# Cross attention of a decoder step: prompt tiles and sample batches in one alternating order, memory keys turned in the projection ahead

## The chip, the cores and the metric

One core of one Trainium2 chip runs the whole program. The metric is device microseconds (us) of that core; lower is better. TensorE (PE, with its weight loads PEld), VectorE (DVE), ScalarE (ACT), GpSimd (POOL) and SyncE (SP, which only issues DMAs here) each run their own instruction list in order and meet at semaphores.

## The reference, cut to what matters

The kernel computes one layer of a decoder for a prompt (512 tokens, 1024 wide) and for 8 sample batches of 8 tokens each. The change lies in its second part, the cross attention into 256 memory tokens with 4 heads of 256:

```python
def memory_attend(h, mk, mv, w_mq, g_q_mem, w_mo):
    q = rmsnorm((h @ w_mq).reshape(B, L, 4, 256), g_q_mem)
    s = jnp.einsum('blhd,bmhd->bhlm', q, mk).astype(F32) * (256 ** -0.5)
    p = jax.nn.softmax(s, axis=-1)
    o = jnp.einsum('bhlm,bmhd->blhd', p, mv.astype(F32)).reshape(B, L, D_MODEL)
    return o.astype(h.dtype) @ w_mo
```

The prompt attends to keys and values projected in this step from `mem_prompt` (they are outputs too); each sample batch attends to keys and values of its own, read from a cache in HBM (256 x 1024 floats each, 1 MB of keys and 1 MB of values a batch, 16 MB in all).

## The kernel before, in words

The program is a row of stages, each a block that all engines enter and leave together: input projection, mixing (retention and windowed attention), output projection, memory projection, `project_cross` (queries), `cross_attend`, `project_back` (the product with `w_mo`), routing, experts. All numbers are float32. Where accuracy allows the fast matrix path, a float32 matrix is split into a high and a low part of type fp32r and three products are summed; the sample batches' own products and all turns (transposes on PE) are plain float32.

`project_cross` (L1300) calls the helper `dense` (L156), which runs the products k = 0 to 9: two blocks of 512 weight columns, each over five row tiles (four of 128 prompt tokens, one of 64 sample tokens). It uses PSUM banks 0 to 3 for products and 4, 5 for turning the inputs, and calls hooks of ACT, DVE and PE after each product. `wide_norm` (L1252) hangs the per-head norm of the queries there: ACT squares (L1266), DVE reduces (L1274), POOL makes the factor (L1293, L1295), DVE scales (L1285, L1286).

`cross_attend` (L1310) then has two halves, one after the other.

The prompt half: fourteen turn groups of four 128 x 128 turns each (`turns`, L1342, issued at L1376): eight of the prompt's queries, four of the memory keys, two of the samples' queries. They go through four PSUM banks; ACT writes the high part (L1490 is the line of its copy helper, so all its copies have it), DVE the low part (L1557) or a plain copy (L1554). ACT and DVE also split the memory values (L1497, L1569). Then for each tile of 128 queries, with the names that are used below:
- S(t): 24 matmuls of scores into banks 2 and 3 (L1388)
- M(t): DVE takes the maxima (L1563, L1565); E(t): ACT makes the exponentials and their sums (L1504); N(t): DVE normalizes (L1573, L1574)
- TP(t): PE turns the probabilities, 8 turns into banks 4 and 5 (L1402), ACT and DVE split them (L1490, L1579)
- O: after every second tile, 48 matmuls with the values (L1415) into banks 6, 7, 0, 1, evicted by ACT in four parts

S(t+1) is issued ahead of TP(t). S has to wait until E of the tile before has read the banks.

The cache half runs the 8 sample batches in loops. For each batch n:
- K(n): 16 turns of the batch's keys in four groups (L1431) into banks 0 and 1, evicted by DVE (L1591) and ACT into one buffer `skt`
- CS(n): scores, small matmuls of 32 columns of queries (L1441); CM(n): maximum on DVE (L1595, L1597); CE(n): exponential on ACT (L1536); CT(n): turn of the probabilities (L1449); CP(n): their eviction on DVE (L1602)
- CV(n): product with the values (L1456); CN(n): normalization on DVE (L1604, L1607); CO(n): turn of the output (L1464); CW(n): its eviction on DVE (L1610)

The order on PE is K(n+1), CT(n), CV(n), CS(n+1), CO(n). SP first stores the two memory outputs, then loads two batches of keys and values; each later load waits until the batch two before has been read (L1361, L1363). The last thing in SP's list is the first 2 MB of `w_mo` (L152, called at L1366); it waits for the O products (L1365), because it overwrites the turned probabilities.

Of the kernel before, what the change touches and what calls it, by code (L numbers as in the profile page):

```python
# [41 lines left out]
P = 128  # L42
# [1257 lines left out]
def project_cross(nc, m, a):  # L1300

    qm = m.at("cross_q", m.Z, [NT, D])
    m.cross_q = qm
    store = lambda act, bank, b, t: act.activation(qm[:rows(t), t, 512 * b:512 * b + 512], bank[:rows(t), :], ACT.Copy)
    widths = [rows(t) for t in range(NT)]
    hooks = wide_norm(nc, m, "cross", None, qm, m.g_q_mem, NT, widths)
    dense(nc, m, "cross", m.x, m.w_mq, range(NT), store, hooks, m.g_cross, widths, m.Z + 10240)


def cross_attend(nc, m, a):  # L1310

    qm, mk, mv = m.cross_q, m.mem_k, m.mem_v
    qt = m.at("cross_q_t", m.Z + 9216, [C8, T])
    sk = [m.at(f"cache_k{i}", m.W + 2048 * i, [2, D]) for i in range(2)]
# [3 lines left out]


    qt_hi, qt_lo = m.at("cross_q_hi", m.HTH, [C8, SEQ], F32R), m.at("cross_q_lo", m.Z + 9216, [C8, T], F32R)  # L1320
    kt_hi, kt_lo = m.at("mem_k_hi", m.Z + 15872, [C8, MEM], F32R), m.at("mem_k_lo", m.Z + 9216 + C8 * T, [C8, MEM], F32R)
    mv_hi, mv_lo = m.at("mem_v_hi", m.Z + 5120, [2, D], F32R), m.at("mem_v_lo", m.Z + 7168, [2, D], F32R)
    pt_hi, pt_lo = (m.at(f"cross_probs_t_{n}", m.Z + 2048 * i, [2 * MH, 2 * P], F32R) for i, n in enumerate(("hi", "lo")))
    spb = [m.at(f"cache_probs{i}", m.WH + 5120 + 256 * i, [MEM]) for i in range(2)]
    S = m.sem
    tr_done, tr_hi, tev = S("cr_turned"), S("cr_turned_hi"), S("cr_turns_out")
    mv_split, pt_h = S("mem_v_split"), S("cr_p_hi")
    sc_done, mx_done, ex_done, pn_done = S("cr_scored"), S("cr_max"), S("cr_exped"), S("cr_normed")
    pt_done, pt_ev, o_done, o_ev = S("cr_p_turned"), S("cr_p_stored"), S("cr_out"), S("cr_out_stored")
    kin, vin = [S("cache_k0_in"), S("cache_k1_in")], [S("cache_v0_in"), S("cache_v1_in")]  # L1330
    qs = m.at("cache_q", m.WH + 5888, [C8, 32])
    ps = m.at("cache_probs_turned", m.WH + 6144, [2, P])
    so = m.at("cache_out", m.WH + 6400, [MD])
    so_done, st_done = m.sem("cs_out_normed"), m.sem("cs_out_turned")
    cq_done = S("cache_q_done")
    ch, stores = S("cr_chain"), S("cr_stores")
    kt_done, kt_ev = S("ck_turned"), [S("ck_stored_even"), S("ck_stored_odd")]
    s_sc, s_mx, s_ex, s_rl = S("cs_scored"), S("cs_max"), S("cs_exped"), S("cs_recip")
    s_pt, s_pev, s_o, s_oev = S("cs_p_turned"), S("cs_p_stored"), S("cs_out"), S("cs_out_stored")
    ckv = [a[n].rearrange("a b (t p) h d -> p (a b) t (h d)", p=P) for n in ("cache_mem_k", "cache_mem_v")]  # L1340

    turns = [(qm, qt_hi, qt_lo, t, j) for t in range(NT - 1) for j in range(2)] + \  # L1342
        [(mk, kt_hi, kt_lo, t, j) for t in range(2) for j in range(2)] + [(qm, None, qt, NT - 1, j) for j in range(2)]
    TURN_BANKS = (0, 1, 6, 7)
    OUT_BANKS = (6, 7, 0, 1)
    four = lambda ap: ap.rearrange("p (c n) -> p c n", c=4)
    NQ = NT - 1
    SC = MD ** -0.5

    with nc.Block() as block:  # L1350
        @block.sync
        def _(sp):
            for src, dst in ((mk, "o_mk"), (mv, "o_mv")):
                sp.dma_start(a[dst].rearrange("a b (t p) h d -> p (a b t) (h d)", p=P), src[:]).then_inc(stores, 16)
            for b in range(2):
                sp.dma_start(sk[b][:], ckv[0][:, b]).then_inc(kin[b], 16)
                sp.dma_start(sv[b][:], ckv[1][:, b]).then_inc(vin[b], 16)
            with sp.Fori(0, NB // 2 - 1) as i:
                for b in range(2):
                    nxt = bass.ds(i * 2 + 2 + b, 1)  # L1360
                    sp.wait_ge(kt_done, i * 8 + 4 * b + 4)  # L1361
                    sp.dma_start(sk[b][:], ckv[0][:, nxt].rearrange("p a t n -> p (a t) n")).then_inc(kin[b], 16)
                    sp.wait_ge(s_o, i * 2 + b + 2)  # L1363
                    sp.dma_start(sv[b][:], ckv[1][:, nxt].rearrange("p a t n -> p (a t) n")).then_inc(vin[b], 16)
            sp.wait_ge(o_done, 4 * (NQ // 2))  # L1365
            m.w_mo.load(sp)  # L1366
            sp.wait_ge(stores, 32)

        @block.tensor
        def _(pe):  # L1370
            for k, (src, _, _, t, j) in enumerate(turns):
                r = rows(t) if src is qm else P
                if k >= 4:
                    pe.wait_ge(tev, k - 3)
                for c in range(4):
                    last = pe.transpose(m.bank[TURN_BANKS[k % 4]][:, c * P:c * P + r],  # L1376
                                        src[:r, t, (4 * j + c) * P:(4 * j + c + 1) * P], m.ident[:r, :r])
                last.then_inc(tr_done, 1)
            pe.wait_ge(tev, len(turns))

            def scores(t):
                if t:
                    pe.wait_ge(ex_done, 4 * t)
                for h in range(MH):
                    o = m.bank[2 + h // 2][:, (h % 2) * MEM:(h % 2 + 1) * MEM]
# [6 lines left out]
            scores(0)  # L1392
            for t in range(NQ):
                if t + 1 < NQ:
                    scores(t + 1)
                pe.wait_ge(pn_done, t + 1)
                if t:
                    pe.wait_ge(pt_ev, 2 * t)
# [5 lines left out]
                if t % 2 == 0:  # L1404
                    continue
# [3 lines left out]
                if t > 1:  # L1409
                    pe.wait_ge(o_ev, 4 * (t // 2))  # L1410
# [959 lines left out]
```

## Time and profile before

| | us |
|---|---|
| median of three runs (lowest to highest) | 1192.34 (1188.83 to 1197.03) |
| the profiled execution's own time | 1192.52 |
| its span, first to last instruction | 1190.7 |
| mean granted TensorE clock, share of full | 0.886 |
| TensorE busy in the span | 931.5 (78%) |
| VectorE, ScalarE busy | 530.2 (45%), 358.0 (30%) |

The span leaves out 1.8 us around the program. The granted clock is the share of 2.4 GHz that TensorE was given; it takes the levels 0.5 (1.2 GHz) and 1.0, and a number between is a mean over time. The rows further down are of three kinds: stretches of the span with each engine's busy time, groups or single instructions in order of their start, and the times that a DMA took from issue to landing. "x8" means eight instructions merged into a row; what stands in brackets is how long the engine had been idle and what ended it.

### The profile page before, as it was taken

To read this page: it belongs to the slowest core of one execution; us is meant where nothing else is said; L and a number is where in the kernel's file an instruction comes from. 1 tells how busy PE (TensorE), PEld (TensorE's weight loads), DVE (VectorE), ACT (ScalarE), POOL (GpSimd) and SP (SyncE) were. 2 spreads that over 40 slices of the span, in tenths; PEclk is the share of its full clock that TensorE was granted. 3 is DMA by queue.
4 is the path that set the end of the run, shared out by engine and by line. 5 is a ranking of instruction groups with operands and counts; after the bars stand their busy time and mean duration, and the time that the engine had idled before them with its cause. 6 is when DMAs were issued, how large, how long until landed. Compare 5 with 4: busy or idle time off the path is not lost. (4 is left out here: it accounts for less than half of the span.)

```text
span 1190.7 us, 14646 instructions
## 1 busy us (share of the span) xinstructions
PE 931.5 (78%) x5762; PEld 653.6 (55%) x5762; DVE 530.2 (45%) x876; ACT 358.0 (30%) x638; POOL 114.7 (10%) x138
## 2 busy tenths in 40 slices
PE   3989999987777777796969777659762999877881
PEld 2877888864554454685758666438652443322330
DVE  3366467335455444335545553454145334223324
ACT  4532234123444444425355243233130011000010
POOL 1000015421000000000212300000010111111000
PEclk9999999967999888797979978999955899888996
DMA  7111217074777665522440050676085699999967
GB/s 247 37 41 65 72 71 167 32 263 124 221 223 220 202 196 160 187 71 71 142 141 1 6 207 1 247 278 252 7 316 229 241 419 420 420 419 422 420 276 254
DMA packets 80132, 231.83 MB, mean 195 GB/s; under 512 B 23104, under 2 KB 23744, under 8 KB 65600
## 3 DMA queue, kind: packets, MB, share of 16 engines
q1 hardware_dynamic: 73008, 220.66, 51.7%
q0 software_dynamic: 4608, 9.45, 2.1%
q10 hardware_dynamic: 2448, 0.80, 0.3%
q8 instruction: 46, 0.75, 0.3%
q14 instruction: 22, 0.18, 0.0%
HBM read 219.46 MB, written 18.74 MB: 200 GB/s over the span
## 5 line engine op out<-in xcount | busy, mean ns | idle before, releaser
L1952 PE MATMUL bank<-gate_up,slot_rows_t 128*64 128x512 f32 x512 | 126.2, 649 | 27.2 <-DMA gate_up<-w_exp_up 25.3
L1952 PEld LDWEIGHTS bank<-gate_up,slot_rows_t 128*64 128x64 f32 x512 | 41.8, 150 | 109.4 <-issue 76.2
L358 PE MATMUL bank<-in_wh,in_hth 128*128 128x512 f32 x224 | 90.7, 405 | 3.1 <-DVE in_wl L302 3.1
L359 PE MATMUL bank<-in_wl,in_hth 128*128 128x512 f32 x224 | 88.9, 397 | 0.0
L360 PE MATMUL bank<-in_wh,in_htl 128*128 128x512 f32 x224 | 88.7, 396 | 0.0
L2159 DVE TENSOR_TENSOR slot_rows_t<-bank,g_moe 128x512 f32<-128x512 f32 x32 | 20.7, 686 | 148.7 <-PE bank L1946 148.7
L862 PE MATMUL bank<-ident,k_half 128*128 128x128 f32 x320 | 53.1, 309 | 26.0 <-ACT window_k_t L992 17.0
L1966 PE MATMUL bank<-down,hidden_t 128*64 128x512 f32 x256 | 58.5, 597 | 8.4 <-issue 7.3
L862 PEld LDWEIGHTS bank<-ident,k_half 128*128 128x128 f32 x320 | 38.7, 154 | 42.5 <-ACT window_k_t L992 22.4
L2112 ACT ACTIVATE swish<-bank 128x256 f32<-128x256 f32 x16 | 6.2, 385 | 177.8 <-PE bank L1952 177.8
L358 PEld LDWEIGHTS bank<-in_wh,in_hth 128*128 128x128 f32 x224 | 43.2, 193 | 12.8 <-issue 3.5
L360 PEld LDWEIGHTS bank<-in_wh,in_htl 128*128 128x128 f32 x224 | 43.0, 192 | 9.4
L359 PEld LDWEIGHTS bank<-in_wl,in_hth 128*128 128x128 f32 x224 | 43.1, 192 | 8.6
L302 DVE TENSOR_TENSOR in_wl<-in_w,in_wh 128x1024 fp32r<-128x1024 f32 x28 | 32.4, 1219 | 21.1 <-ACT in_wh L235 21.1
L435 ACT ACTIVATE z<-bank 128x512 f32<-128x512 f32 (+1 forms) x35 | 20.5, 589 | 69.3 <-PE bank L360 58.0
L1123 DVE COPY window_k_t<-bank 128x512 f32<-128x512 f32 x40 | 27.5, 688 | 29.3 <-PE bank L862 29.3
L970 ACT ACTIVATE probs<-scored,att_max 128x128 f32<-128x128 f32 (+3 forms) x32 | 17.7, 554 | 74.4 <-DVE att_max L1108 74.4
L1966 PEld LDWEIGHTS bank<-down,hidden_t 128*64 128x64 f32 x256 | 20.2, 136 | 35.6 <-issue 35.6
L208 POOL TENSOR_SCALAR stat<-stat 128x1 f32<-128x1 f32 (+1 forms) x12 | 3.0, 248 | 332.3 <-ACT mem_normed L224 263.1
L235 ACT ACTIVATE in_wh<-in_w 128x1024 fp32r<-128x1024 f32 x28 | 27.3, 1045 | 21.2 <-DMA in_w<-w_in 21.2
L1936 POOL DMA_INDIRECT slot_rows<-moe_rows_dram,slot_token x16 | 16.5, 1029 | 160.6 <-PE bank L1946 104.4
L358 PE MATMUL bank<-wo_wh,wo_hth 128*128 128x512 f32 x64 | 26.2, 410 | 5.9 <-DVE wo_wl L302 5.9
(386 smaller groups left out, 2048.9 us busy)
## 6 DMA issues: line engine op xcount, KB each, us to landing
gate_up<-w_exp_gate SPq DMA_DIRECT2D x32, 1024.0 KB, 21.2
gate_up<-w_exp_up SPq DMA_DIRECT2D x32, 1024.0 KB, 24.9
down<-w_exp_down SPq DMA_DIRECT2D x32, 1024.0 KB, 23.1
in_w<-w_in SPq DMA_DIRECT2D x7, 2048.0 KB, 8.3
k_half<-cache_win_k SPq DMA_DIRECT2D x48, 256.0 KB, 6.2
v_half<-cache_win_v SPq DMA_DIRECT2D x48, 256.0 KB, 4.9
k_half<-cache_win_k SPq DMA_DIRECT2D x8, 1024.0 KB, 6.0
v_half<-cache_win_v SPq DMA_DIRECT2D x8, 1024.0 KB, 8.4
```

Of the source, the lines that this page charges most:

```text
L235: act.activation(wh[b % 2][:, part(i)], w[b % 2][:, part(i)], ACT.Copy).then_inc(wh_done, 1)
L302: dve.tensor_tensor(wl[b % 2][:, part(i)], w[b % 2][:, part(i)], wh[b % 2][:, part(i)].bitcast(F32), ALU.subtract).then_inc(wl_done, 1)
L358: pe.matmul(o, hi, wh[b % 2][:, c, :], start=(c == 0), stop=False)
L359: pe.matmul(o, hi, wl[b % 2][:, c, :], start=False, stop=False)
L360: last = pe.matmul(o, lo, wh[b % 2][:, c, :], start=False, stop=(c == C8 - 1))
L435: return act.activation(z[ZB[b]][:rows(t), t, :], bank[:rows(t), :], ACT.Copy)
L862: last = pe.transpose(m.bank[KBANK[c % 2]][:, q * P:(q + 1) * P], win.k[part][:, c % HC, q * P:(q + 1) * P], m.ident[:, :])
L970: act.activation(pb[:, e, :n], sb[:, e, :n], ACT.Exp, bias=m.amx[:, c], accum_out=m.asum[:, c]).then_inc(ex_done, 1)
L1123: dve.tensor_copy(kt[:, :, c * P:(c + 1) * P], m.bank[KBANK[0]][:].rearrange("p (q n) -> p q n", q=NP)).then_inc(kt_ev[0], 1)
L1952: last = pe.matmul(bank[64 * h:64 * h + 64, :], B.xt[k % 2][:, c, 64 * h:64 * h + 64], B.gu[k % 3][h][:, :, c, :], start=(c == 0), stop=(c ...
L1966: last = pe.matmul(m.bank[4 + j][64 * h:64 * h + 64, :], B.hidt[n % 2][:, k, 64 * h:64 * h + 64], B.dn[n % 3][h][:, k, 512 * j:512 * j + 5 ...
L2159: dve.tensor_tensor(B.xt[k % 2][:, 4 * j:4 * j + 4, :], four(m.bank[j][:]), over(m.g_moe[:, 4 * j:4 * j + 4], P), ALU.mult).then_inc(xt_ev, 1)
```

## The change

In `project_cross`, the four turn groups of the memory keys, their split and the split of the memory values are hung into the hooks: a turn group behind each of the products k = 4 to 7 (PE, into banks 6 and 7, free there; ACT and DVE each one part of the split), half of the values' split behind k = 7 and k = 8. SP's list of this stage gets the stores of the two memory outputs and, once five products are done, the loads of the keys of batches 0 and 1.

In `cross_attend`, the loops are gone and both halves are issued in one order. Six turn groups (the queries of tile 0, of the samples and of tile 1, without bank reuse) come first; those of tiles 2 and 3 come at the ends of iterations 0 and 1. An iteration t holds tile t and the batches 2t and 2t+1. The sample batches get bank 6 (scores and turned probabilities side by side) and bank 7 (output and turned output); O uses banks 4 and 5 twice. The probabilities and queries of the batches have two buffers. The sum for the normalization of each batch lies in a slot of its own.

```diff
 def project_cross(nc, m, a):
+    TURN_AT, TURNS, SPLIT_AT = 4, 4, 7
...
+    def tensor(pe, k):
+        i = k - TURN_AT
+        if 0 <= i < TURNS:
+            t, j = divmod(i, 2)
+            if i >= 2:
+                pe.wait_ge(lo_done, i - 1)
+            for c in range(4):
+                last = pe.transpose(m.bank[6 + i % 2][:, c * P:(c + 1) * P], mk[:, t, (4 * j + c) * P:(4 * j + c + 1) * P], m.ident[:, :])
+            last.then_inc(turned, 1)
...
+    def later(sp, mm_done):
+        for src, dst in ((mk, "o_mk"), (mv, "o_mv")):
+            sp.dma_start(a[dst].rearrange("a b (t p) h d -> p (a b t) (h d)", p=P), src[:]).then_inc(stores, 16)
+        sp.wait_ge(mm_done, NT)
+        for i in range(2):
+            sp.dma_start(m.cache_k[i][:], m.cache_rows[0][:, i]).then_inc(m.cache_k_in[i], 16)
+        sp.wait_ge(stores, 32)
...
 def cross_attend(nc, m, a):
+    turns = [(0, 0), (0, 1), (NQ, 0), (NQ, 1), (1, 0), (1, 1), (2, 0), (2, 1), (3, 0), (3, 1)]
+    turn_bank = (0, 1, 6, 7, 2, 3, 4, 5, 4, 5)
+    EARLY = 6
...
         def _(sp):
+            for n in range(2):
+                sp.dma_start(sv[n][:], rows_of[1][:, n]).then_inc(vin[n], 16)
+            for n in range(2, NB):
+                sp.wait_ge(kt_done, 4 * (n - 1))
+                sp.dma_start(sk[n % 2][:], rows_of[0][:, n]).then_inc(kin[n % 2], 16)
+                sp.wait_ge(s_o, n - 1)
+                sp.dma_start(sv[n % 2][:], rows_of[1][:, n]).then_inc(vin[n % 2], 16)
             sp.wait_ge(o_done, 4 * (NQ // 2))
             m.w_mo.load(sp)
...
+            def turn_q(k):
...
+                if k in (6, 7):
+                    pe.wait_ge(pt_ev, 2)
+                if k in (8, 9):
+                    pe.wait_ge(o_ev, 4)
...
+            def outputs(t, j):
+                if j < 2:
+                    pe.wait_ge(pt_ev, 2 * t + 2)
+                else:
+                    pe.wait_ge(o_ev, 4 * (t // 2) + j - 1)
...
+            for k in range(EARLY):
+                turn_q(k)
+            scores(0)
+            keys(0)
+            for t in range(NQ):
+                n = 2 * t
+                cache_scores(n)
+                if t:
+                    cache_out(n - 1)
+                keys(n + 1)
+                cache_turn(n)
+                turn_probs(t)
+                cache_values(n)
+                if t + 1 < NQ:
+                    scores(t + 1)
+                cache_scores(n + 1)
+                if t + 1 < NQ:
+                    keys(n + 2)
+                cache_out(n)
+                if t % 2:
+                    outputs(t, 0)
+                    outputs(t, 1)
+                cache_turn(n + 1)
+                if t % 2:
+                    outputs(t, 2)
+                    outputs(t, 3)
+                if t + 2 < NQ:
+                    turn_q(EARLY + 2 * t)
+                    turn_q(EARLY + 2 * t + 1)
+                cache_values(n + 1)
+            cache_out(NB - 1)
...
         def _(act):
+            for k in range(EARLY):
+                q_high(k)
+            keys(0)
+            exps(0)
+            for t in range(NQ):
+                n = 2 * t
+                cache_exps(n)
+                keys(n + 1)
+                probs_high(t)
                 if t + 1 < NQ:
                     exps(t + 1)
+                cache_exps(n + 1)
+                if t + 1 < NQ:
+                    keys(n + 2)
                 if t % 2:
                     for j in range(4):
+                        store_outputs(t, j)
+                if t + 2 < NQ:
+                    q_high(EARLY + 2 * t)
+                    q_high(EARLY + 2 * t + 1)
...
         def _(dve):
+            put_q(0)
+            put_q(1)
+            maxima(0)
+            keys(0)
+            norm_probs(0)
+            for t in range(NQ):
+                n = 2 * t
+                cache_maxima(n)
+                if t:
+                    cache_store(n - 1)
+                keys(n + 1)
+                cache_probs(n)
+                if t + 1 < NQ:
+                    put_q(n + 2)
+                probs_low(t)
+                cache_norm(n)
                 if t + 1 < NQ:
                     maxima(t + 1)
+                cache_maxima(n + 1)
+                if t + 1 < NQ:
+                    keys(n + 2)
+                cache_store(n)
+                if t + 1 < NQ:
+                    norm_probs(t + 1)
+                cache_probs(n + 1)
+                if t + 1 < NQ:
+                    put_q(n + 3)
+                if t + 2 < NQ:
+                    q_low(EARLY + 2 * t)
+                    q_low(EARLY + 2 * t + 1)
+                cache_norm(n + 1)
+            cache_store(NB - 1)
```

## Rows read from the trace of the kernel before

**Rows 1.** Stretches: us, busy (x) of PE, PEld, DVE, ACT, POOL, clock, DMA, GB/s
```profile
654.00:676.00 22.00, 22.00 (x98) 17.93 (x96) 11.83 (x18) 6.03 (x10) 9.78 (x12) 1.00 0.00 0
...
683.40:693.80 10.40, 8.79 (x57) 7.23 (x57) 8.39 (x15) 8.68 (x13) 0.00 (x0) 0.83 0.93 343
693.80:744.20 50.40, 36.03 (x224) 34.51 (x224) 18.87 (x29) 16.63 (x49) 0.00 (x0) 0.77 0.14 55
744.20:799.30 55.10, 37.76 (x416) 24.63 (x416) 26.90 (x80) 13.88 (x33) 0.00 (x0) 1.00 0.73 267
```

**Rows 2.** Timeline, end of cross_attend and start of project_back
```profile
799.02 0.29 DVE L1610 COPY ht<-bank 128x32 f32<-128x32 f32 x2 [0.53 <-PE bank L1464]
...
800.57 3.88 ACT L235 ACTIVATE back_wh<-back_w 128x1024 fp32r<-128x1024 f32 x4
...
803.20 0.77 PE L358 MATMUL bank<-back_wh,back_hth 128*128 128x512 f32 x1 [4.22 <-DVE back_wl L302]
```

**Rows 3.** Timeline, the turns at the start of cross_attend
```profile
683.47 5.54 PE L1376 MATMUL bank<-ident,cross_q 128*128 128x128 f32 x32 [7.41 <-PEq L192]
...
687.00 3.69 DVE L1557 TENSOR_TENSOR cross_q_lo<-bank,cross_q_hi 128x512 fp32r<-128x512 f32 x6 [0.16 <-ACT cross_q_hi L1490]
...
693.79 0.58 PE L1388 MATMUL bank<-mem_k_hi,cross_q_hi 128*128 128x256 f32 x1 [1.40 <-DVE cross_q_t L1554]
```

**Rows 4.** Timeline, one prompt tile: TP(0), M(1), E(1), N(1), S(2)
```profile
707.08 1.04 PE L1402 MATMUL bank<-ident,cross_probs 128*128 128x128 f32 x8
707.27 1.42 DVE L1563 TENSOR_REDUCE att_max<-bank 128x2 f32<-128x512 f32 x2 [3.89 <-PE bank L1388]
...
708.93 0.47 ACT L1504 ACTIVATE cross_probs<-bank,att_max 128x256 f32<-128x256 f32 x1
...
711.11 1.23 DVE L1574 TENSOR_TENSOR cross_probs<-cross_probs,att_sum 128x1024 f32<-128x1024 f32 x1
```

**Rows 5.** PE at L1388 alone, S at either clock: us, PE, PEld, clock
```profile
701.80:707.00 5.20, 5.13 (x24) 5.13 (x24) 0.50 0.00 0
724.00:726.90 2.90, 2.84 (x24) 2.89 (x24) 1.00 0.00 0
```

**Rows 6.** PE at L1415 alone, the first 48 O products: us, PE, PEld, clock
```profile
718.10:724.10 6.00, 5.90 (x48) 5.82 (x48) 1.00 0.00 0
```

**Rows 7.** Timeline, one batch of the cache half (seven more are like it)
```profile
748.49 1.07 PE L1441 MATMUL bank<-cache_k_t,cache_q 128*32 128x256 f32 x16 [0.73 <-DVE cache_k_t L1591]
...
749.49 1.09 PE L1431 MATMUL bank<-ident,cache_k 128*128 128x128 f32 x8
749.62 0.42 DVE L1595 TENSOR_REDUCE win_stat<-bank 128x1 f32<-128x256 f32 x1 [1.57 <-PE bank L1441]
...
750.27 0.47 ACT L1536 ACTIVATE cache_probs<-bank,win_stat 128x256 f32<-128x256 f32 x1 [1.87 <-DVE win_stat L1597]
750.36 0.69 DVE L1591 COPY cache_k_t<-bank 128x512 f32<-128x512 f32 x1
...
751.11 1.09 PE L1431 MATMUL bank<-ident,cache_k 128*128 128x128 f32 x8 [0.52 <-DVE cache_k_t L1591]
...
752.04 0.38 PE L1449 MATMUL bank<-ident,cache_probs 128*128 128x128 f32 x2
...
752.46 0.42 DVE L1602 COPY cache_probs_turned<-bank 128x256 f32<-128x256 f32 x1
...
753.02 1.07 PE L1456 MATMUL bank<-cache_v,cache_probs_turned 128*32 128x256 f32 x16 [0.60 <-DVE cache_probs_turned L1602]
...
754.23 0.48 DVE L1607 TENSOR_SCALAR cache_out<-bank,win_stat 128x256 f32<-128x256 f32 x1 [1.27 <-PE bank L1456]
...
754.88 0.44 PE L1464 MATMUL bank<-ident,cache_out 128*128 128x128 f32 x2
```

**Rows 8.** Timeline, SP's issues of the two w_mo loads, merged
```profile
787.20 12.76 SPq L152 DMA_DIRECT2D back_w<-w_mo  x2
```

**Rows 9.** The same two loads: from issue to landing
```profile
DMA to landing us min/median/max: 8.0/8.9/9.7
```

More of the change, by code:

```diff
@@ new lines, in scalar @@
+    def scalar(act, b, t, stored, k):
+        norm["scalar"](act, b, t, stored, k)
+        i = k - TURN_AT
+        if 0 <= i < TURNS:
+            act.wait_ge(turned, i + 1)
+            act.activation(part(m.kt_hi, i), four(m.bank[6 + i % 2][:]), ACT.Copy).then_inc(hi_done, 1)
+        if SPLIT_AT <= k < SPLIT_AT + 2:
+            i = k - SPLIT_AT
+            if i == 0:
+                act.wait_ge(stores, 32)
+                act.wait_ge(turned, TURNS)
+            act.activation(m.mv_hi[:, i, :], mv[:, i, :], ACT.Copy).then_inc(v_hi_done, 1)
@@ L1346, in cross_attend, with turned_part @@
+    NQ = NT - 1
+    turns = [(0, 0), (0, 1), (NQ, 0), (NQ, 1), (1, 0), (1, 1), (2, 0), (2, 1), (3, 0), (3, 1)]
+    turn_bank = (0, 1, 6, 7, 2, 3, 4, 5, 4, 5)
+    EARLY = 6
+    KEYS, SCORES, PT, SAMPLE, SAMPLE_OUT = (0, 1), (2, 3), (4, 5), 6, 7
     four = lambda ap: ap.rearrange("p (c n) -> p c n", c=4)
-    NQ = NT - 1
+    two = lambda ap: ap.rearrange("p (c n) -> p c n", c=2)
     SC = MD ** -0.5
+    def turned_part(k, dst):
+        t, j = turns[k]
+        r = rows(t)
+        return four(m.bank[turn_bank[k]][:])[:, :, :r], dst[:, 4 * j:4 * j + 4, t * P:t * P + r]
@@ L1480, in _ @@
-            turn_out(NB - 1)
-        def turned_part(k, dst):
-            src, _, _, t, j = turns[k]
-            r = rows(t) if src is qm else P
-            return four(m.bank[TURN_BANKS[k % 4]][:])[:, :, :r], dst[:, 4 * j:4 * j + 4, t * P:t * P + r]
+            for k in range(EARLY):
[28 more added lines that the diff above has]
+                cache_values(n + 1)
@@ L1490, in _, with q_high @@
             copy = lambda dst, src: act.activation(dst, src, ACT.Copy)
[L1491 to L1492 removed]
+            def q_high(k):
+                if turns[k][0] < NQ:
                     act.wait_ge(tr_done, k + 1)
[L1494 removed]
+                    got, dst = turned_part(k, qt_hi)
                     copy(dst, got).then_inc(tr_hi, 1)
[L1496 to L1497 removed]
             def exps(t):
@@ L1514, in _, with store_outputs, keys @@
                         act.wait_ge(o_done, 4)
-                    copy(pt_hi[:, 4 * j:4 * j + 4, tc], four(m.bank[4 + j][:])).then_inc(pt_h, 1)
+                    copy(pt_hi[:, 4 * j:4 * j + 4, t % 2 * P:(t % 2 + 1) * P], four(m.bank[PT[j]][:])).then_inc(pt_h, 1)
+            def store_outputs(t, j):
+                act.wait_ge(o_done, 4 * (t // 2) + j + 1)
+                copy(m.ht[:, 2 * j:2 * j + 2, (t - 1) * P:(t + 1) * P], two(m.bank[PT[j % 2]][:])).then_inc(o_ev, 1)
+            def keys(n):
+                if n:
+                    act.wait_ge(s_sc, n)
+                for k in range(1, 4, 2):
+                    t, j = divmod(k, 2)
+                    act.wait_ge(kt_done, 4 * n + k + 1)
+                    copy(skt[:, 4 * j:4 * j + 4, t * P:(t + 1) * P], four(m.bank[KEYS[1]][:])).then_inc(kt_ev[1], 1)
```

331 lines of the change are left out of this document (150 added, 181 removed).

## The prediction

> **What bounds the kernel now.** I read the page's busy shares first: TensorE leads with 78%, so no engine is full over the whole span. Then I cut the span into the stretches that the change touches [rows 1]. In the projection ahead TensorE is busy for the whole 22.00 us: whatever is added for it there costs its full length, while DVE (11.83) and ACT (6.03) have room. In cross_attend it is the other way round. The prompt half has TensorE busy 36.03 of 50.40 us, and at a mean clock of 0.77; the cache half 37.76 of 55.10 us at clock 1.00. DVE and ACT are busy for half of either or less. So this stage is a chain of hand-overs between three engines, in two halves that know nothing of each other, and that is where something can be won. From its first turn at 683.47 [rows 3] to the first product of the next stage at 803.20 [rows 2] it takes 119.7 us. All engines meet at the end of each stage, and everything behind starts relative to that point, so I carry what this stretch gains to the end one to one.
>
> **How much work there is.** At full clock a S takes 2.9 us [rows 5], so four take 11.6; the O products 2 x 5.9 = 11.8 [rows 6]; a K of 16 turns about 2 x 0.9 without the drain at its end (8 take 1.09 with it), CS 1.0, CV 0.9, CT and CO 0.25 each [rows 7]: 4.2 a batch, 33.6 for eight; 32 turns of TP 3.8 and 10 turn groups of queries 4.2. That is 65 us of TensorE for the stage after the change: a floor, if nothing ever waited.
>
> **The walk through the new order.** I follow the three lists and start each step when its engine is free and its input is there, with the distances of the trace. CM starts 1.13 after CS, CE 0.65 after CM, CP 0.42 after CT, CN 1.21 after CV, CO 0.65 after CN; a third turn group of K comes 0.75 after the start of the copy that frees its bank [rows 7]. M starts 0.2 after the last matmul of S, E 1.66 after M, the scaling in N 2.18 after E and takes 1.23, so that TP can come 3.4 after the start of E [rows 4].
>
> Prologue, from the stage's start: fourteen turn groups end in S(0) after 10.3 us now. The eight that go (four of keys, four of queries) run at the fast pace, 3.69 / 6 = 0.615 each on DVE [rows 3]: 4.9 less, and 0.6 more for memset and the missing overlap. S(0) at 6.0, at a clock that is mostly low: until 9.5. M(0) 9.7. DVE copies the first quarter of K(0) only behind M(0), at 11.35; K(0) is on PE until 13.0, its last eviction until 13.8, CS(0) at 13.9. E(0) stands behind those copies on ACT, 13.8 to 15.8, N(0) until 17.3, and CM(0) behind N(0). That is 16.2 behind the stage's start where the steady order has it at 1.13, and with the following steps iteration 0 behaves as if it began at 16.0. The split of the values (one DVE instruction of 2.3 us between M(0) and N(0) now) is gone from here.
>
> Iteration 0, times from its CS(0): CM 1.1, K(1) on PE 1.3 to 3.65 (its third group waits for DVE, which does CM first), CT 3.7, TP 3.9, CP 4.2, CV 4.85, S(1) 5.75 to 8.6, CS(1) to 9.55, half of K(2) to 10.4. Here DVE is late: M 8.8, CM 10.4, first copy of K(2) 10.95; and ACT later: E 10.4 to 12.3, CE, copy until 13.5. So the fourth group of K(2) is at 13.6, CO and CT until 14.55; DVE writes out, does N (15.1 to 16.55) and CP until 17.0; CV(1) 17.1 to 18.0. The query turns of 0.9 us fit into the gap before CV. Iteration 0: 18.0 us, in which PE works for 13.
>
> Iteration 1 is the same until 14.5; then O, four parts of 1.45 and the CT between them, until 20.5. The two turn groups behind need banks 4 and 5, which ACT has emptied at 21.4: turns 21.5 to 22.4, CV to 23.3. Iteration 2: 18.0, and 0.4 because DVE is still at the query parts: 18.4. Iteration 3 has no S, M, E, N or K behind it: O runs from 7.5 to 13.6, CV to 14.4, the last write ends at 16.3.
>
> **What is late next: the load of w_mo.** SP waits for the last O with it. Now O is finished 43 us before SP gets there, the load goes at 787.20 [rows 8] and is hidden by the last batches. In the new order O ends 2.7 us before the end of the stage. Two megabytes land 8.0 to 9.7 us after issue [rows 9]; the 8.0 is the one with no load ahead of it, so I take that. Issue at 16.0 + 18.0 + 23.3 + 18.4 + 13.65 = 89.35; landed 97.35; ACT's first split 0.1 later; the first product 2.63 after that (800.57 to 803.20 [rows 2]): 100.1. Without this wait ACT would split 1.26 after the last write [rows 2], at 93.25, so it costs 4.2. Against 119.7: 19.6 less.
>
> **The projection.** PE gets 16 turns, in four groups behind full products: 8 take 1.09 with one drain [rows 7], so 4 x 0.45 = 1.8, and nothing hides it [rows 1]. DVE gets four parts of 0.69 and the 2.3 of the values, ACT 4 x 0.6 and 1.9: about 5 and 4.3 us into 10 and 16 us of idle time. DVE's second half of the values falls just ahead of its part in the last product: 0.3. PE's third and fourth group wait for DVE's low parts, which are one product (5.4 us) ahead. Together 2.1 us; from 1.8, if all of DVE's part is covered, to 4, if a group waits. SP's two stores and two key loads move here, into time without DMA (share 0.00 [rows 1]): nothing. The keys of batch 0 are there when K(0) comes; before, they were as well.
>
> **Loads of the batches.** Each later load of keys stands in SP's list behind a load of values that waits for a CV. The tightest is that of batch 6: its values ahead (batch 5) wait for the CV that ends iteration 1, so both go out at the start of iteration 2, and K(6) wants its keys 9.9 later; 2 MB land in 8.0 to 9.7 [rows 9]. Batch 4 is alike in iteration 1. I charge nothing; the other end is 1 us in each of the two.
>
> **The clock.** S takes 5.2 us at 0.50 and 2.9 at 1.00 [rows 5]. In the prompt half the clock was low after each longer idle of PE; in the cache half, with an idle in every batch, it stayed at 1.00 for 55 us [rows 1]. The new order is like the latter, but has thin stretches (PE at work for 1.6 of 7 us from 10.4 on) in the even iterations and a thin prologue. Bounds: 0, if it holds, and 13 (S four times 2.3, and as much again on half of the small steps of two iterations). I take 3: one S, and a TP or CV. On clock the Trainium skill (TensorE: Matmul & The Clock Gate, section "A second HAM failure mode: psum-queue depth-cycling") says that brief idles between groups, as PE goes round its PSUM banks, can make the clock drop and return over and over. By that rule the whole stage would run as the prompt half did; the trace agrees for that half (0.77) and disagrees for the cache half (1.00), which is why it is a rival below and not the sum.
>
> **Sum.** -19.6 + 2.1 + 3.0 = -14.5. From the profiled execution's 1192.52 that gives 1178.0; the median of the runs, 1192.34, is 0.2 from it, so I leave it there. A measurement of this kernel can tell about 1% (12 us) from no change: the bound for faster is 1180.4.
>
> **The rivals.**
> - The clock holds throughout, as it did in the cache half, and my steps, each rounded up, are short by some tenths: 1192.5 - 17.5 - 3 = 1172. For it: 55 us at 1.00. Against: the prologue is thinner than any batch was.
> - The queues couple more than the walk says. ACT's and DVE's lists are in order, and each K eviction stands behind an E, M or N of up to 1.9 us; where one step slips, all three lists do. At 2 us in each of four iterations: 1186. For it: in the walk DVE or ACT ends the wait at five places of an iteration. Against: DVE, the fuller of them, has 54.2 us of work in the stage now [rows 1], 49 without what moves away, of 92.
> - Slower: the clock stays at 0.50 in most of the stage, because between 10.4 and 17 of every iteration PE does little, and the next dense part is slow before it is granted again. Price: S and O double, 9 and 10 us, and of the 42 us of turns and small products the part that is on the path, about 60%, doubles too, 25: at most 44. It decides from 17.5 on, when 40% of that is taken; at 60%, 26 us, the time is 1201. Against: the cache half.
> - It doesn't hide: the loads of the batches land late, one after another, and the alternating order runs at their pace: Their 14 MB take 55 us at the 267 GB/s that the cache half moved [rows 1], so bandwidth alone doesn't bind in 92; it binds if loads are issued too late. Then 4 us in each of three iterations: 1190.
>
> **How the numbers follow.** Forecast 0.50 (its own range 1173 to 1184), clock holds 0.18, queues couple 0.22, slower 0.06, loads 0.04. Faster by over 1%: two thirds of the forecast, all of the second, a little of the third: 0.34 + 0.18 + 0.04 = 0.56. Slower by over 1%: the slow clock alone, 0.05. Within 1%: 0.39. The range 1170 to 1190 leaves out the slow clock, the ends of the loads' case and a gain above 22 us.
>
> **What would show it.** Right: cross_attend from first turn to last write in some 92 to 96 us; iterations of about 18, 23, 18 and 16; an idle of ACT of about 4 us ended by DMA back_w at its start of project_back; the projection 2 us longer; PE waiting in iteration 0 for DVE's CP behind N. Wrong: a mean clock of cross_attend under 0.8; PE waiting for DMA cache_k or cache_v; K evictions that wait for E; the w_mo wait absent, or over 6 us; a projection more than 4 us longer.

## The result and the profile after

The changed kernel takes 1175.59 us (median of 4 executions, 1173.72 to 1176.29) beside 1190.59 for the one before (4 executions): a ratio of 0.9853 [0.9823, 0.9882], faster by 1.5%. Forecast was 1178.0, in a range of 1170 to 1190, and faster by over 1% had the larger chance. The execution that was profiled took 1173.72, its span is 1171.9.

Five stretches of the two profiled executions, in us. A stretch ends where the next begins, at the row named:

| stretch | before | after | difference |
|---|---|---|---|
| all stages ahead of project_cross | 607.59 | 605.32 | -2.27 |
| project_cross, until the first query turn | 75.88 | 77.87 | +1.99 |
| cross_attend, until the first product of project_back | 119.73 | 102.04 | -17.69 |
| from there to the experts' first product | 122.66 | 118.99 | -3.67 |
| to the end of the span | 264.84 | 267.68 | +2.84 |

The two lines in the middle are the change: -15.7. The first line and the last two are stages in which the programs are alike; they move by some us in either direction and make up the rest of the -18.8. The last section has what the traces show of that.

First the page of the changed kernel:

```profile
span 1171.9 us, 14468 instructions
PE 920.2 (79%) x5762; PEld 643.4 (55%) x5762; DVE 529.4 (45%) x878; ACT 357.5 (31%) x639; POOL 114.8 (10%) x138
```

The busy shares hardly differ from before (PE 78%). Only a cut by stretches shows something. The windows of the changed kernel (us, busy (x) of PE, PEld, DVE, ACT, POOL, clock, DMA share, GB/s): one stretch of the projection, then the stage's turns and S(0), iterations 0 to 3, and the whole stage to its last write. Iterations 1 to 3 are counted from their CS; iteration 0 from 1.13 ahead of its CM(0) at 699.68, the distance of the steady order:

```profile
653.20:675.40 22.20, 22.20 (x105) 18.19 (x103) 14.12 (x22) 9.87 (x16) 8.29 (x11) 1.00 0.11 41
683.19:693.00 9.81, 8.27 (x55) 7.59 (x56) 4.61 (x11) 2.34 (x4) 0.00 (x0) 0.79 0.59 215
...
698.55:717.30 18.75, 13.54 (x120) 10.91 (x122) 11.60 (x26) 7.39 (x20) 0.00 (x0) 0.91 0.39 149
717.30:741.81 24.51, 21.46 (x196) 17.97 (x192) 11.38 (x29) 9.80 (x24) 0.00 (x0) 0.93 0.46 172
741.81:760.29 18.48, 13.91 (x140) 10.12 (x136) 11.27 (x30) 6.32 (x18) 0.00 (x0) 0.96 0.62 229
760.29:777.20 16.91, 15.17 (x150) 11.51 (x142) 6.92 (x21) 5.80 (x12) 0.00 (x0) 0.94 0.25 79
683.19:777.20 94.01, 75.73 (x680) 60.38 (x680) 48.28 (x120) 34.68 (x88) 0.00 (x0) 0.92 0.44 160
```

Against [rows 1]: the two halves and their turns took 115.8 us together from first turn to last write; now it is 94.01, with TensorE busy 81% of it. The window of the kernel before over the same part is:

```profile
683.47:799.30 115.83, 82.57 (x696) 66.33 (x696) 54.16 (x124) 39.20 (x93) 0.00 (x0) 0.88 0.49 182
```

So of the 21.8 us that went, 15.0 are time in which PE did nothing (33.3 before, 18.3 now) and 6.8 are busy time: there are 16 turns fewer, and the clock is 0.92 for 0.88.

In the projection PE is full as before, DVE and ACT do more. The iterations last 18.75, 24.5, 18.5 and 16.9; forecast were 18.0, 23.3, 18.4 and 16.3.

The prologue, in the timeline (start, duration, engine, line, operation, and in brackets the idle time before and what ended it); it answers to [rows 3] and to the first of [rows 7]:

```profile
683.19 4.57 PE L1434 MATMUL bank<-ident,cross_q 128*128 128x128 f32 x24 [7.62 <-PEq L192]
...
689.30 0.39 PE L1450 MATMUL bank<-mem_k_hi,cross_q_hi 128*128 128x256 f32 x1 [1.54 <-DVE cross_q_lo L1636]
...
692.27 1.03 PE L1487 MATMUL bank<-ident,cache_k 128*128 128x128 f32 x8
692.47 1.42 DVE L1648 TENSOR_REDUCE att_max<-bank 128x2 f32<-128x512 f32 x2 [3.03 <-PE bank L1450]
...
694.00 0.68 DVE L1670 COPY cache_k_t<-bank 128x512 f32<-128x512 f32 x1
694.74 1.09 PE L1487 MATMUL bank<-ident,cache_k 128*128 128x128 f32 x8 [1.44 <-DVE cache_k_t L1670]
...
696.57 1.07 PE L1496 MATMUL bank<-cache_k_t,cache_q 128*32 128x256 f32 x16 [0.73 <-DVE cache_k_t L1670]
...
698.54 1.23 DVE L1656 TENSOR_TENSOR cross_probs<-cross_probs,att_sum 128x1024 f32<-128x1024 f32 x1
```

S(0) starts 6.1 behind the first turn instead of 10.3 [rows 3]. K(0)'s first copy stands behind M(0) on DVE at 694.00, and CS(0) starts at 696.57, 13.4 behind the first turn. N(0) is in DVE's way at 698.54, and CM(0) is pushed behind it: it starts at 699.68.

The end of iteration 0, on PE, answers to [rows 4] and [rows 7] in the mixed order:

```profile
709.79 1.09 PE L1487 MATMUL bank<-ident,cache_k 128*128 128x128 f32 x8
711.70 0.66 PE L1487 MATMUL bank<-ident,cache_k 128*128 128x128 f32 x4 [0.82 <-DVE cache_k_t L1670]
713.48 0.66 PE L1487 MATMUL bank<-ident,cache_k 128*128 128x128 f32 x4 [1.13 <-ACT cache_k_t L1558]
713.97 0.38 PE L1521 MATMUL bank<-ident,cache_out 128*128 128x128 f32 x2
714.19 0.38 PE L1503 MATMUL bank<-ident,cache_probs 128*128 128x128 f32 x2
714.41 1.04 PE L1434 MATMUL bank<-ident,cross_q 128*128 128x128 f32 x8
716.41 1.07 PE L1513 MATMUL bank<-cache_v,cache_probs_turned 128*32 128x256 f32 x16 [0.97 <-DVE cache_probs_turned L1685]
```

K waits here first for DVE's copy, which stands behind M and CM, then for ACT's, behind E and CE; and CV(1) waits for CP, which stands behind N. These are the hand-overs that the walk had named.

The end of the stage, where before nothing waited for the weights [rows 2, 8]:

```profile
774.77 3.07 SPq L152 DMA_DIRECT2D back_w<-w_mo  x2
...
776.88 0.29 DVE L1699 COPY ht<-bank 128x32 f32<-128x32 f32 x2 [0.53 <-PE bank L1521]
...
782.77 3.90 ACT L235 ACTIVATE back_wh<-back_w 128x1024 fp32r<-128x1024 f32 x4 [4.23 <-DMA back_w<-w_mo]
```

Last, PE's groups of the stage by line, where time was idle ahead of them (busy us, mean ns, idle us and its releasers):

```profile
L1487 PE MATMUL bank<-ident,cache_k 128*128 128x128 f32 x128 | 18.8, 288 | 10.8 <-DVE cache_k_t L1670 7.5 <-ACT cache_k_t L1558 3.4
...
L1513 PE MATMUL bank<-cache_v,cache_probs_turned 128*32 128x256 f32 x128 | 9.3, 411 | 2.8 <-DVE cache_probs_turned L1685 2.8
...
L1521 PE MATMUL bank<-ident,cache_out 128*128 128x128 f32 x16 | 3.4, 296 | 1.3 <-DVE cache_out L1694 1.3
```

Of the 18.3 us in which PE does nothing between first turn and last write, 10.8 stand ahead of key turns. No wait is put down to a load of keys or values. In the kernel before two key groups did wait for their load, 0.21 and 1.53 us, in batches that [rows 7] does not show ("seven more are like it" holds for the steps, and not for this wait):

```profile
769.56 1.09 PE L1431 MATMUL bank<-ident,cache_k 128*128 128x128 f32 x8 [1.53 <-DMA cache_k<-cache_mem_k]
```

The same wait is 3.1 us in keys_ahead_only and 3.4 in unrolled_only, which keep the old order, and absent in order_only: a small part of what the new order gains is loads that now come in time.

### The profile page after: what moved, and what is told of

Same layout as the page of the kernel before. It is cut to its first block and busy times, and to the rows that moved or that the text cites. A ratio compares the mean times of both kernels' runs of the same rounds, so it can differ in the third digit from the quotient of the medians.

```text
span 1171.9 us, 14468 instructions
## 1 busy us (share of the span) xinstructions
PE 920.2 (79%) x5762; PEld 643.4 (55%) x5762; DVE 529.4 (45%) x878; ACT 357.5 (31%) x639; POOL 114.8 (10%) x138
## 5 line engine op out<-in xcount | busy, mean ns | idle before, releaser
L970 ACT ACTIVATE probs<-scored,att_max 128x128 f32<-128x128 f32 (+3 forms) x32 | 17.7, 553 | 74.3 <-DVE att_max L1108 74.3
L358 PE MATMUL bank<-back_wh,back_hth 128*128 128x512 f32 x64 | 26.0, 406 | 8.4 <-DVE back_wl L302 8.4
## 6 DMA issues: line engine op xcount, KB each, us to landing
down<-w_exp_down SPq DMA_DIRECT2D x32, 1024.0 KB, 23.3
```

Of the source, the lines that this page charges most:

```text
L358: pe.matmul(o, hi, wh[b % 2][:, c, :], start=(c == 0), stop=False)
```

## The experiments

**One part at a time.** Three kernels each keep one part of the change. A fourth is the changed kernel once more. keys_ahead_only has the new projection, and the cross_attend of before without its key turns, its split of the values, its two stores and its first two key loads. unrolled_only is the kernel before with its loop over batches written out:

```diff
-with sp.Fori(0, NB // 2 - 1) as i:
+for i in range(NB // 2 - 1):
```

(the same on PE, ACT and DVE). order_only is the changed kernel with the key turns, both splits, the two stores and the first key loads back in cross_attend; the key turns stand behind the first six turn groups of queries and ahead of S(0):

```diff
 def vector(dve, b, t, stored, k):
     norm["vector"](dve, b, t, stored, k)
-    i = k - TURN_AT
...
+for i in range(4):
+    dve.wait_ge(mkh, i + 1)
+    dve.tensor_tensor(kpart(kt_lo, i), four(m.bank[KT_BANK[i]][:]), ...)
...
+dve.wait_ge(mvh, 1)
+dve.tensor_tensor(mv_lo[:], m.mem_v[:], mv_hi[:].bitcast(F32), ALU.subtract).then_inc(mkl, 1)
```

changed_again:

> The changed kernel once more, beside the parts below on one chip. Theory: 14 to 16 us faster than before; of the stretch from the first turn of cross_attend to the first product of project_back 102 us, in it 4.2 us of ScalarE waiting for w_mo. If the gain came from the chip or the moment, the ratio would leave 0.985 by more than 0.004.

keys_ahead_only:

> Before, with only the projection part of the change: the key turns, the splits, the two stores and the first key loads hang in project_cross, the two halves of cross_attend stay one after the other and looped. Theory (the order is the gain): the projection 2.0 us longer, the start of cross_attend four turn groups of 0.6 us shorter, nothing else: within 1.5 us of before. Rival (a good part of the gain is the work moved out of the stage): 4 us or more faster.

unrolled_only:

> Before, with only the loops over the sample batches written out, in the old order. Theory: each pass loses the 0.2 to 0.4 us that engines idle at a loop's turn, and part of that is hidden: 0 to 2 us faster in all. Rival (the loops were what made a batch take 6.4 us): 5 us or more faster, which would take that much from the alternating order.

order_only:

> The changed kernel with the key turns, the splits of keys and values, the two stores and the first key loads back in cross_attend, and the alternating order as it is. Theory: four turn groups of 0.6 us and 2.3 us of DVE for the values ahead of the first K eviction cost 4 to 5 us there, the projection is 2.0 shorter: 2 to 3 us slower than the changed kernel, 12 to 13 faster than before. Rival (without keys turned ahead the order is worth little): under 8 us faster than before.

Measured, with the lengths of the two stretches in the profiled execution:

| kernel | us | ratio to before | projection | cross_attend until the product |
|---|---|---|---|---|
| before | 1190.76 | | 75.88 | 119.73 |
| changed_again | 1174.21 | 0.9864 [0.9838, 0.9891] | 77.81 | 101.97 |
| keys_ahead_only | 1191.66 | 1.0000 [0.9975, 1.0025] | 78.03 | 118.47 |
| unrolled_only | 1191.67 | 1.0006 [0.9982, 1.0031] | 75.66 | 120.33 |
| order_only | 1173.80 | 0.9857 [0.9833, 0.9880] | 75.72 | 104.76 |

The order, with the banks, the second buffers and the written-out code that it needs, makes the whole gain. Beside the kernel before, order_only has the same 696 matmuls in cross_attend:

```profile
681.67:778.30 96.63, 77.74 (x696) 61.44 (x696) 53.16 (x125) 38.69 (x93) 0.00 (x0) 0.91 0.54 199
```

PE is idle for 18.9 us of it instead of 33.3, and busy for 77.74 instead of 82.57. So 14.4 of the 19.2 us from first turn to last write are shorter waits, and 4.8 are busy time of the same work; the clock, 0.91 for 0.88, accounts for most of these (an estimate from the busy time at clock 0.50, 21.3 us before and 14.8 now: 3.3).

unrolled_only, expected to be 0 to 2 us faster, came out no faster. Its trace shows two things at once: up to CS(5) its batches run 2.4 us faster than the looped ones (29.24 us from CS(0) for 31.59); then K waits 1.84 us for its load and the clock is 0.50 from 782.2 to 789.0, as it never was in that half of the kernel before, and the gain is gone. So writing the loops out gives nothing by itself here, but some 2 us of the new order's gain may be theirs; no run takes that apart.

The keys ahead cost 2.1 in the projection and give back 1.3 in the old order, 2.8 in the new one: nothing that the median can tell, in either. For order_only I had expected 2 to 3 us more than the changed kernel. Its two stretches together are 0.7 longer (180.5 against 179.8), its median is 0.4 shorter. DVE's timeline and PE's show what the keys cost there:

```profile
695.45 2.29 DVE L1707 TENSOR_TENSOR mem_v_lo<-mem_v,mem_v_hi 128x2048 fp32r<-128x2048 f32 x1
697.65 0.69 DVE L1662 COPY cache_k_t<-bank 128x512 f32<-128x512 f32 x1
698.39 1.97 PE L1465 MATMUL bank<-ident,cache_k 128*128 128x128 f32 x8 [3.64 <-DVE cache_k_t L1662]
```

The split of the values stands in DVE's list between M(0) and K(0)'s first copy, and PE waits 3.64 instead of 1.44. CS(0) comes 19.4 behind the first turn, 6.0 later than in the changed kernel. But 1.75 of that come back at once: K(1)'s third group waits 0.55 for DVE there and 2.30 in the changed kernel, where N(0) is in its way. Another 1.5 come back in iteration 1 (23.04 for 24.51 us): the changed kernel runs the first part of its O at clock 0.52 there (row 731.90 further down), order_only at 1.00. By CS(4) the distance is 2.9, at the first product 2.7. So a late prologue is partly taken up by the chain behind it, and partly it was the clock that fell elsewhere.

**The wait for w_mo.** Block 0 of w_mo goes to words that are free once S(3) is done and the last batch's queries are copied, so that its load need not wait for the last O; the experts' load behind it waits for project_back's own products, since those words are theirs:

```diff
-sp.wait_ge(o_done, 4 * (NQ // 2))
+sp.wait_ge(sc_done, NQ)
+sp.wait_ge(q_put, NB)
...
-m.w_mo = Weights(..., (m.Z, m.Z + 4096), ...)
+m.w_mo = Weights(..., (m.Z + 10240, m.Z + 4096), ...)
```

> The changed kernel with the first half of w_mo in memory that is free after S(3), loaded at the start of iteration 3; the first expert loads wait until the first block of project_back is done. Theory: ScalarE's wait of 4.2 us for w_mo goes, 4 us faster than the changed kernel. Rival (something else ends last there, or the late expert loads cost it at the end): no gain or a loss, with the wait gone from the row.

Measured: 1174.61, ratio 0.9858 [0.9810, 0.9905]; from first turn to the product 97.88, so 4.15 less. ACT goes from its split of the inputs to that of the weights with no wait, since the load left 17 us ahead of that:

```profile
766.41 0.42 SPq L152 DMA_DIRECT2D back_w<-w_mo  x1
...
782.85 1.06 ACT L241 ACTIVATE back_hth<-ht 128x1024 fp32r<-128x1024 f32 x1 [2.10 <-PEq L1411]
783.81 3.88 ACT L235 ACTIVATE back_wh<-back_w 128x1024 fp32r<-128x1024 f32 x4
```

So within the stage the wait of 4.23 was on the path in full, and the later loads of the experts cost nothing that shows (385.3 us from the product to the end, 384.9 to 386.7 in the three traces of the changed kernel). The median did not show it: it lies near the changed kernel's, which was not run beside it, and this profiled execution came to project_cross at 610.70, 5.4 later than the changed kernel's. So both once more, side by side:

> The changed kernel a third time, as the base for the three beside it, on one chip. Theory: the median within 1174 to 1176, the projection ahead starting near 605 us as in its two traces so far.

> w_mo_early again, because its stage was 4.1 us shorter in the trace and its median no better. In that trace project_cross started 5.4 us later than in the changed kernel, behind stages that are the same in both. Theory (that is the clock in those stages, which differs from one execution to the next): it starts elsewhere this time and the median is 3 to 5 us under the changed kernel's. Rival (it belongs to this program and comes each time): it starts near 610.7 again and the median equals the changed kernel's.

Measured: changed_beside 1176.14 (0.9865 [0.9833, 0.9897]), w_mo_early_2 1170.82 (0.9817 [0.9792, 0.9843]): 5.3 less, with a stage of 97.85 against 102.03. The stage accounts for 4.2 of it. On the late start both expectations missed: w_mo_early_2 came to project_cross at 610.94, as the rival had it (whose equal median is not what was measured), and changed_beside at 610.07, where 605 was expected of it. all_three, with the same edit, comes there at 605.66 and 606.82. So the late start is not due to the edit; it comes with the execution.

**The hand-overs.** In cp_first DVE does CP ahead of N. In copies_ahead each half of K's copies also goes ahead: DVE's first copy ahead of CM, ACT's ahead of E, and the second ones stay behind; in the prologue E(0) goes ahead of ACT's second copy of K(0).

```diff
 # cp_first, DVE
+cache_probs(n + 1)
 norm_probs(t + 1)
-cache_probs(n + 1)
 # copies_ahead, ACT and DVE as well
+keys(n + 2, (1,))
 exps(t + 1)
 cache_exps(n + 1)
-keys(n + 2)
+keys(n + 2, (3,))
```

> The changed kernel with one swap on VectorE: CP(n+1) ahead of N(t+1). Theory: TensorE's waits for CP before CV (1.0 and 1.8 us in iterations 0 and 2) shrink by the 1.4 us of N: 2 to 3 us faster than the changed kernel. Rival (iterations are bound by TensorE's own work, or N is then late for TP): within 1 us.

> As cp_first, and the first copy of each K on ScalarE ahead of E, the first copy on VectorE ahead of CM, in the prologue E(0) ahead of the second copy. Theory: TensorE's waits inside K after S (0.8 and 1.1 us) go in three iterations and the prologue shrinks by 1.8: 6 to 8 us faster than the changed kernel. Rival (the three lists push each other, and E is now the late one): no better than cp_first.

Measured: cp_first 1172.77 (0.9856 [0.9804, 0.9908]), stage 99.11, 2.9 less, which its median does not tell from the changed kernel; copies_ahead 1164.45 (0.9766 [0.9720, 0.9813]), stage 92.24, 9.8 less, where 6 to 8 were expected. PE's groups by line, cp_first:

```profile
L1513 PE MATMUL bank<-cache_v,cache_probs_turned 128*32 128x256 f32 x128 | 8.6, 385 | 0.5 <-DVE cache_probs_turned L1685 0.5
L1521 PE MATMUL bank<-ident,cache_out 128*128 128x128 f32 x16 | 3.4, 292 | 2.5 <-DVE cache_out L1694 2.4
```

and copies_ahead, with its windows (the first 3.5 us, and all behind until the last write):

```profile
L1487 PE MATMUL bank<-ident,cache_k 128*128 128x128 f32 x128 | 17.3, 278 | 4.3 <-DVE cache_k_t L1672 4.3
...
L1521 PE MATMUL bank<-ident,cache_out 128*128 128x128 f32 x16 | 3.3, 290 | 2.5 <-DVE cache_out L1696 2.3
L1503 PE MATMUL bank<-ident,cache_probs 128*128 128x128 f32 x16 | 3.2, 280 | 2.6 <-ACT cache_probs L1599 2.6
```

```profile
686.09:689.60 3.51, 3.51 (x19) 3.06 (x20) 2.07 (x5) 1.19 (x2) 0.00 (x0) 0.50 0.61 217
689.60:770.30 80.70, 67.27 (x663) 53.57 (x661) 46.44 (x116) 32.89 (x86) 0.00 (x0) 1.00 0.49 178
```

The account for copies_ahead closes: idle ahead of K falls by 6.5 and ahead of CV by 2.3, ahead of CT and CO it rises by 2.6 and 1.2, so 5.0 less waiting. PE's busy time falls from 75.73 to 70.77, by 5.0 too, with the same instructions: that is the clock, which now stays at 1.00 from the end of the turns on. Together 10.0 of the measured 9.8. What was expected had only the waits in it. In cp_first: 2.3 less, 1.2 more, and 1.7 of busy time (74.07 in its stage) make 2.8 of 2.9.

**All of them.** all_three is copies_ahead (which holds cp_first) with w_mo_early:

> w_mo_early and copies_ahead together. Theory: they lie at different places, so they add: 10 to 12 us faster than the changed kernel, near 1164 us. Rival (the low clock comes more often as the stage gets shorter, or w_mo lands late again): under 8 us.

> all_three again, for the same question as w_mo_early_2. Theory: a median of 1160 to 1162. Rival: 1164 again, as copies_ahead.

Measured: 1164.05 (0.9778 [0.9725, 0.9832]) and, once more, 1163.79 (0.9772 [0.9745, 0.9800]); stage 87.96 and 87.98, that is 14.0 less than the changed kernel, the sum of 9.8 and 4.15. In the stage the two edits add up in full. Over the median all_three has not been told from copies_ahead (1164.45), though its stage is 4.3 shorter: its first six executions spread from 1159 to 1174, and the repeat, expected at 1160 to 1162, came near the rival's 1164. From the product to the end the two traces of all_three take 385.9 and 388.7 us, that of copies_ahead 385.8: once the 4.3 reach the end, once most of them are lost behind the stage. That they reach it as a rule is likely from w_mo_early_2's median, and not shown for this pair.

**The clock.** filled has extra turns of the unit matrix, in the waits of K and ahead of CV, whose results nobody reads (89 more matmuls than in the changed kernel's records). They stand inside the waits: the time in which PE does none of its own matmuls is 18.2 us of the stage, for 18.3 in the changed kernel. What they change is PE's clock:

```diff
+def fill(bank, many):
+    for _ in range(many):
+        pe.transpose(m.bank[bank][:, 0:P], m.ident[:, :], m.ident[:, :])
...
-keys(n + 2)
+keys(n + 2, (6, 8))
```

> The changed kernel with extra turns of the identity, whose results nobody reads, where TensorE waits: 10 in K(0), 16 in K(1), 14 in each later K behind S, 7 and 14 ahead of CV in iterations 0 and 2. Nothing else differs, and they fit into the waits. Theory (the thin stretches are what costs the clock): the mean clock of cross_attend rises from 0.92 to 0.97 or more, and the stage is 2 to 3 us shorter. Rival (the clock falls whatever stands in the waits, or low clock costs nothing as TensorE waits anyway): the same length or longer.

Measured: 1168.98 (0.9809 [0.9774, 0.9843]), stage 97.18: 4.85 less, where 2 to 3 were expected. Stretches of the changed kernel that were slow, then filled's from the end of its first turns on:

```profile
683.19:686.70 3.51, 3.51 (x19) 3.06 (x20) 2.07 (x5) 1.20 (x2) 0.00 (x0) 0.50 0.67 207
...
701.50:704.20 2.70, 2.70 (x14) 2.70 (x13) 1.22 (x3) 0.60 (x1) 0.00 (x0) 0.50 0.00 0
...
731.90:735.20 3.30, 3.30 (x18) 3.30 (x17) 1.50 (x4) 0.88 (x2) 0.00 (x0) 0.52 0.00 0
...
758.90:762.20 3.30, 3.30 (x33) 1.35 (x29) 0.48 (x1) 0.00 (x0) 0.00 (x0) 0.51 0.16 19
```

```profile
683.11:686.70 3.59, 3.59 (x19) 3.14 (x20) 2.15 (x5) 1.19 (x2) 0.00 (x0) 0.50 0.61 224
686.70:773.00 86.30, 77.13 (x752) 63.19 (x750) 46.10 (x116) 33.73 (x87) 0.00 (x0) 1.00 0.47 168
```

The three stretches behind the turns are gone. The rows hold 9.3 us of full PE at half speed, and 10.2 with the edges that they leave out (PE is busy there too): at full speed that is 4.65 to 5.1 us less, and 4.85 were measured. The 680 matmuls that both kernels have cover 71.0 us in filled and 75.73 in the changed kernel, so the gain is in their own speed and not in a wait.

## Why the prediction was right

- **The stage.** Forecast were 103.1 from first turn to first product; it took 102.04. From first turn to last write 92 to 96 were named, it is 94.01. order_only and keys_ahead_only show that this comes from the order, as the walk had it, and the new order's waits stand at the places that the walk named (CP behind N; copies of K behind M, CM and E). One of the signs of being wrong, "K evictions that wait for E", is there as well: PE waits 3.4 us for ACT's copies behind E. The walk itself has that step (fourth group of K(2) at 13.6), so the sign contradicts the walk; it says nothing against the order, and taking it away is part of what copies_ahead gains.
- **The prologue.** CS(0) was forecast at 13.9 behind the first turn; it came at 13.4. Iteration 0 behaves as if begun at 15.36, for 16.0: turns and S(0) took 9.1 instead of 9.5.
- **The iterations.** 18.75, 24.5, 18.5 and 16.9 sum to 78.65; forecast were 76.0 without the clock. The excess of 2.65 is near the 3.0 that stood beside it as the clock's term. They are alike by chance, as the next point shows.
- **The term that was too small: "The clock ... I take 3: one S, and a TP or CV."** Two stretches were charged; there were three behind the turns (a K group with TP, the first part of O, CV with CS), none of them an S, and filled shows 4.85 for them. That the sum still came out is luck: the walk's own steps were long by about 2.9 (100.1 without the clock's term, against 97.18 in filled), 0.6 of it in the prologue, and the two errors cancel in part. The rival in which it holds throughout is not what happened to this kernel; filled and copies_ahead are what it would have been. The slow rival never came near: 0.92 over the stage, 0.88 before. The term of 3 was a charge against a walk at full clock; beside the kernel before, the clock was a gain. The Trainium skill (TensorE: Matmul & The Clock Gate, section "A second HAM failure mode: psum-queue depth-cycling") has the clock go down and up with brief idles between groups. Here it did so three times in 94 us, each time behind two or three waits of PE of 0.7 to 2.3 us, and the trace agrees as to the kind. It cost 5 us and not the whole stage, and at the end of iteration 0 three like waits (0.82, 1.13 and 0.97) did not lower it; which waits do lower it is not shown by these traces.
- **The wait for w_mo.** 4.2 was forecast, 4.23 measured; w_mo_early removes it, and the stage is 4.15 shorter. This was the one new wait that the kernel got, and the landing of 8.0 taken from the other place held.
- **The projection.** +2.1 forecast, +1.99 measured (keys_ahead_only 2.15 over before, order_only 2.15 under the changed kernel). PE's four groups cost about 0.45 each as said. DVE's half of the values does stand ahead of its part in the last product:

```profile
675.39 1.23 DVE L1353 TENSOR_TENSOR mem_v_lo<-mem_v,mem_v_hi 128x1024 fp32r<-128x1024 f32 x1
676.53 0.68 DVE L321 TENSOR_TENSOR bank<-bank,ht 64x512 f32<-64x512 f32 x1
```

- **The loads.** No wait of PE for keys or values; charged nothing, and that was right. What the walk did not see is that the kernel before had such waits, 1.7 us, in its cache half, and that the new order would end them.
- **The floor.** PE's work was put at 65 us. copies_ahead is busy for 70.8 in the stage, and 68.7 if its first turns at half clock are counted at full (an estimate): about 4 too low. Nothing in the sum rests on it.
- **The sum.** Both stretches together were forecast at -14.5 and came to -15.7. On the medians the change is -15.0 (1190.59 to 1175.59). Of the 2.4 between 1178.0 and 1175.59, 1.75 is the median before, which lay lower over four executions than over three, 0.2 that I began from 1192.52, and 0.5 the change.
- **What I would now say otherwise.** The prediction treats the change as one. It should have split the sum by parts: -15 for the order and almost nothing for the keys ahead. The walk had numbers for the latter, 2.1 to pay and four turn groups of 0.615 and a split of 2.3 to gain, but never followed the order with a prologue that is 4.8 longer.

## What to carry to other kernels

When two halves of a stage each wait for hand-overs, alternate them, and write the walk down for each engine's own list: who is late is found by the step that stands ahead in an in-order list, and moving the late step past its neighbour can be worth more than half of the interleaving itself (9.8 us of the stage beside 17.7 here, for a few moved lines; half of the 9.8 is the clock). When a stage gets shorter, look at the load behind it, which was hidden by the part that shrank: 4.2 us here. A change in PE's idle pattern moves its clock, and for such a stage the clock should be a term of the sum with its own count of low stretches.

## What the runs showed of the hardware beyond this

**Work whose results nobody reads made the stage shorter.** filled issues 89 more matmuls, and the stage loses 4.85 us, since the clock stays at 1.00. Behind the stage its trace gives some of that back: from the first product of project_back to the experts' it took 122.43 against 118.99, and a window from PE's last product of project_back to the experts' first shows a clock of 0.53 in 69.0 us, against 0.57 in 65.9 for the changed kernel:

```profile
833.71:902.72 69.01, 28.71 (x229) 25.42 (x227) 31.46 (x87) 12.65 (x19) 6.36 (x15) 0.53 0.65 239
```

It does not take extra turns for this. The kernel before, which has none, needs 122.66 for the stretch, and its window is like filled's:

```profile
857.10:925.86 68.76, 28.35 (x227) 25.40 (x227) 31.43 (x87) 12.66 (x19) 6.37 (x15) 0.55 0.65 240
```

What decides between the 65.9 and the 69.0 us was not tried. filled's median is 7.2 below that of changed_beside all the same.

**The same instructions don't take the same time in each execution.** Ahead of project_cross all these programs are alike, and their profiled executions reach it between 604.6 and 610.9 us. The stretch from 300 to 400 us, in the changed kernel and in w_mo_early:

```profile
300.00:400.00 100.00, 74.48 (x837) 50.26 (x840) 49.26 (x111) 45.87 (x113) 0.00 (x0) 0.92 0.72 214
```

```profile
300.00:400.00 100.00, 77.31 (x834) 51.97 (x832) 49.61 (x115) 43.30 (x108) 0.00 (x0) 0.86 0.74 220
```

The three latest (changed_beside at 610.1, w_mo_early at 610.7, its repeat at 610.9) have 0.90, 0.86 and 0.86 there, copies_ahead at 608.3 has 0.86, and those with 0.92 or 0.93 lie between 604.6 and 608.2. So the clock there goes with the four latest, and leaves 3.6 us between the others unexplained. Over all 16 executions of the changed kernel the times spread from 1168 to 1180, with a mean of 1175.2; w_mo_early's 12 have a mean of 1172.5, all_three's 12 one of 1164.2. The length of cross_attend in contrast came out at 102.04, 101.97 and 102.03 in three executions. For a part of some us, the stretch in the trace tells what the median of six can't. The Trainium skill (TensorE: Matmul & The Clock Gate, section "Part 1: The HAM clock gate") says that the number of slow matmuls at a kernel's start varies from run to run. These traces agree that the clock of the same code varies, here in mid-program too: 0.86 to 0.93 in one stretch.
